# A hybrid attention and HGRN2 block: the output projection by Strassen's seven products from the second tile of positions on

## The reference, cut to what matters

```python
h = rmsnorm(x, w_norm_pre)
proj = h @ w_in                         # (2048, 1024) @ (1024, 3328)
q_a, k_a, v_a, z_a, q_r, f_r, i_r, z_r = split(proj)
o_a = sliding_window_sink_attention(rope(q_a), rope(k_a), v_a, sinks) * silu(z_a)   # 512 columns
o_r = rmsnorm(hgrn2_chunkwise(q_r, f_r, i_r, lb)) * silu(z_r)                       # 512 columns
y = concatenate([o_a, o_r]) @ w_out     # (2048, 1024) @ (1024, 1024)
x = x + rmsnorm(y, w_norm_post)
```

## Time and profile before

| what | value |
|---|---|
| time, median of 3 runs | 876.72 us (874.83 to 877.73) |
| the profiled execution | span 872.4 us from first to last instruction; its own time is not listed apart from the three runs |
| median of the runs less the span | 4.3 us |
| PE busy | 862.6 us, 4478 matmuls |
| DVE, ACT, POOL busy | 592.9, 499.3, 115.7 us |
| DMA | 186 MB, mean 213 GB/s |

### The profile page before, as it was taken

How to read it: one execution, slowest core, us unless ns; L and a number is a source line. 1 busy time by engine, 2 the same in 40 slices (tenths; PEclk the granted TensorE clock), 3 DMA queues, 4 the chain that set the end, 5 groups by cost and what they waited for, 6 DMA issues and landing times.

```text
span 872.4 us, 12348 instructions
## 1 busy us (share of the span) xinstructions
PE 862.6 (99%) x4478; PEld 709.9 (81%) x4478; DVE 592.9 (68%) x1061; ACT 499.3 (57%) x1009; POOL 115.7 (13%) x90
## 2 busy tenths in 40 slices
PE   8999999999999999999999999999999999999997
PEld 6887788888888788888888878888888877788886
DVE  6878867764756798867163679878625468977823
ACT  7766456663574559657147546866624655667532
POOL 0000013430200001342020000243111000013112
PEclk9999999999999999999999999999999999999999
DMA  8685755639968544552785644446379545444463
GB/s 319 236 307 205 265 199 180 250 145 365 418 229 286 221 170 145 177 185 99 289 328 201 241 172 166 146 146 211 130 262 338 193 147 176 154 151 146 161 245 126
DMA packets 52924, 186.03 MB, mean 213 GB/s; under 512 B 5888, under 2 KB 6144, under 8 KB 52864
## 3 DMA queue, kind: packets, MB, share of 16 engines
q1 hardware_dynamic: 50128, 178.29, 57.2%
q10 hardware_dynamic: 2736, 6.95, 2.0%
HBM read 141.18 MB, written 44.04 MB: 212 GB/s over the span
## 4 chain that ended last, share of the span: by engine, by line
PE 88%; DVE 5%; DMA 3%; ACT 2%; issue 1%; SPq 1%; POOL 0%; DVEq 0%; ACTq 0%
PE bank L478 61%; PE bank L487 8%; PE score_b L487 4%; PE turn_b L487 4%; DMA kept_lo<-w_lo 2%; PE score_b L507 2%; PE turn_b L531 2%; PE turn_b L584 2%; PE bank L565 2%; PE turn_b L587 1%; PE bank L575 1%; DVE q_gate L1305 1%; PE turn_b L521 1%; DMA x_in<-in_x 1%; DVE w_lo L997 1%
## 5 line engine op out<-in xcount | busy, mean ns | idle before, releaser
L478 PE MATMUL bank<-h_hi,w_lo 128*128 128x512 f32 x832 | 327.1, 393 | 0.0
L478 PE MATMUL bank<-h_lo,w_hi 128*128 128x512 f32 x832 | 325.9, 392 | 0.0
L478 PE MATMUL bank<-h_hi,w_hi 128*128 128x512 f32 x832 | 324.5, 391 | 0.8 <-ACT h_hi L790 0.8
L478 PEld LDWEIGHTS bank<-h_lo,w_hi 128*128 128x128 f32 x832 | 156.3, 188 | 34.5 <-issue 3.3
L478 PEld LDWEIGHTS bank<-h_hi,w_hi 128*128 128x128 f32 x832 | 156.3, 188 | 33.6 <-ACT h_hi L790 1.3
L478 PEld LDWEIGHTS bank<-h_hi,w_lo 128*128 128x128 f32 x832 | 156.2, 188 | 33.1 <-issue 0.2
L1341 POOL TENSOR_TENSOR mix_lo<-v_r,mix_hi 128x512 fp32r<-128x512 f32 x16 | 21.2, 1323 | 522.6 <-ACT v_r L911 522.6
L997 DVE TENSOR_TENSOR w_lo<-w_raw,w_hi 128x1024 fp32r<-128x1024 f32 x37 | 45.8, 1248 | 32.8 <-ACT w_hi L736 32.6
L1119 DVE STREAM_TRANSPOSE kv_tok<-k_mid 32x128 f32<-32x128 f32 x192 | 58.0, 302 | 2.8
L736 ACT ACTIVATE w_hi<-w_raw 128x1024 fp32r<-128x1024 f32 x38 | 39.7, 1050 | 22.1 <-issue 9.9
L487 PE MATMUL bank<-w_hi,mix_lo 128*128 128x512 f32 x128 | 50.5, 395 | 0.0
(11 more groups left out here) (189 smaller groups left out, 1467.4 us busy)
## 6 DMA issues: line engine op xcount, KB each, us to landing
w_hi<-kept_hi SPq DMA_DIRECT2D x96, 512.0 KB, 3.7
w_lo<-kept_lo SPq DMA_DIRECT2D x96, 512.0 KB, 4.7
w_raw<-in_weights SPq DMA_DIRECT2D x38, 512.0 KB, 5.4
kept_hi<-w_hi SPq DMA_DIRECT2D x34, 512.0 KB, 6.5
kept_lo<-w_lo SPq DMA_DIRECT2D x34, 512.0 KB, 7.1
x_in<-in_x_rows SPq DMA_DIRECT2D x8, 1024.0 KB, 7.2
x_in<-in_x SPq DMA_DIRECT2D x15, 512.0 KB, 5.9
out<-q_gate ACTq DMA_DIRECT2D x9, 512.0 KB, 8.5
```

Of the source, the lines that this page charges most:

```text
L478: mm = pe.matmul(acc(w)[:, :], stationary[:, s, k, :], moving[:, k, :], start=(m == 0), stop=(m == 3 * KT - 1), skip_group_check=True)
```

## The change

Tile 0 is as before. From tile 1 on the 512 positions and the 1024 inputs and 1024 outputs are halved, so that the product is one of 2 by 2 blocks, and seven products of halves take the place of eight. The code has Winograd's form of it, with sums that run on in the banks. `s_hi`, `s_lo` hold three sums of the recurrent and attention halves (S1, S2, S4), `mix_hi[:, 0:4]` the half A11 and the difference S3; they take over the place of `w_raw` in SBUF (with two more slots' room). Of the weights, B11, B21, B12, B22 and four differences T1 to T4 are needed: 14 weight tiles of 1 MiB (high and low) for a tile's output in place of 8, in the order P1A, P1B, P7A, P7B, P2A, P6A, P4A, P2B, P6B, P4B, P5A, P5B, P3A, P3B. The differences are made once, in tile 1, by POOL and ACT from raw weights (`load_sums`, `sum_weights`, `sums_high`) and saved to DRAM (`save_sums`).

One unit is the 3 matmuls of one k block and one 128 positions; there are 56 units (168 matmuls) for a tile. P2B, P6B and P4B are interleaved; P3 finishes the first 128 positions of a half before the second.

```diff
+FAST_ROWS = [B11, B11 + 1, T3, T3 + 1, B21, T2, T4, B21 + 1, T2 + 1, T4 + 1, T1, T1 + 1, B22, B22 + 1]
+FAST_WT = OUT0 + len(FAST_ROWS)
+SPLIT_SLOT = SPLIT_SLOT + [w % 4 for w in range(FAST_WT)] * (TILES - FAST)
+UNITS = [(w, k, i) for w, ks in ((P1A, (0, 1)), (P1B, (2, 3)), (P7A, (0, 1)), (P7B, (2, 3)), (P2A, (0, 1)), (P6A, (0, 1)), (P4A, (0, 1)))
+         for k in ks for i in range(2)]
+UNITS += [(w, k, i) for k in (2, 3) for w in (P2B, P6B, P4B) for i in range(2)]
+UNITS += [(P5A, k, i) for k in (0, 1) for i in range(2)] + [(P5B, k, i) for i in range(2) for k in (2, 3)]
+UNITS += [(w, k, i) for i in range(2) for w, ks in ((P3A, (0, 1)), (P3B, (2, 3))) for k in ks]
...
+SUMS_IN, SUMS_OUT = (6, 13), (11, 18)
+SUMS_AT = (5, 11)
...
+            def load_sums(j):
+
+                if j == 0:
+                    sp.wait_ge(lo_split.sem, lo_split.after(0, 0) + FRESH - 1)
+                else:
+                    sp.wait_ge(t_saved, 16 * T_TILES)
+                for r, w in enumerate((B11, B21, B12, B22)):
+                    sp.dma_start(w_raw[:, r, :, :], weights[(w + j) * P:(w + j + 1) * P, :].rearrange("p (k m) -> p k m", k=KT)).then_inc(t_raw, 16)
+
+            def save_sums(j):
+
+                sp.wait_ge(t_high, 4 * (j + 1))
+                sp.wait_ge(t_low, 4 * (j + 1))
...
-                    if w == WT - 3:
+                    if t == FAST and w in SUMS_IN:
+                        load_sums(SUMS_IN.index(w))
+                    if t == FAST and w in SUMS_OUT:
+                        save_sums(SUMS_OUT.index(w))
+                    if w == (P3A if t >= FAST else WT - 3):
                         load_residual(t, 0)
-                    if w == WT - 1:
+                    if w == tiles_of(t) - 1:
                         load_residual(t, 1)
...
+            def out_fast(t):
+
+                for n, (w, k, i) in enumerate(UNITS):
+                    for part, mix, weight, into in unit(t, w, k, i):
+                        m = 3 * n + part
+                        between(t, OUT0 + m // 21, m % 21)
+                        if part == 0:
+                            unit_waits(t, n, w, k, i)
+                        mm = pe.matmul(into, mix, weight, start=w in (P1A, P7A, P2A, P4A) and k == 0 and part == 0,
+                                       stop=k == KT // 2 - 1 and part == 2, skip_group_check=True)
+                    if w not in [v for v, _, _ in UNITS[n + 1:]]:
+                        mm.then_inc(tile_done.sem, 1)
+                    elif w in (P6B, P5B, P3B) and k == KT // 2 - 1 and i == 0:
+                        mm.then_inc(half_done.sem, 1)
...
+            def sum_head(t, h):
...
+                dve.tensor_tensor(s_tmp[:, S2, :], h_mix[:, 2 * P:], s3[:, h, :], ALU.subtract).then_inc(s_step, 1)
+                dve.tensor_tensor(s_tmp[:, S1, :], h_mix[:, 2 * P:], a21[:, h, :], ALU.add)
+                dve.wait_ge(s_step, (t - FAST) * HEADS + h + 1)
+                dve.tensor_tensor(s_tmp[:, S4, :], h_mix[:, 0:2 * P], s_tmp[:, S2, :], ALU.subtract).then_inc(s_made.sem, 1)
...
+            def sum_weights(j):
+
+                raw = lambda r: w_raw[:, r, :, :]
+                pool.wait_ge(t_raw, 64 * (j + 1))
+                for k, (dst, a, b) in enumerate(((0, 2, 0), (2, 3, 2), (3, 3, 0), (1, 1, 3))):
+                    if k > 1:
+                        pool.wait_ge(t_sum, 4 * j + k)
+                    pool.tensor_tensor(raw(dst), raw(a), raw(b), ALU.subtract).then_inc(t_sum, 1)
+                for k, r in enumerate((0, 2, 3, 1)):
+                    pool.wait_ge(t_high, 4 * j + k + 1)
```

More of the change, by code:

```diff
@@ L57, with index, where, tiles_of @@
 SPLIT_SLOT = [s for r in (4, 4, 4, 4, 4, 4, 4, 3, 3) for s in range(r)]
[L58 to L59 removed]
+FAST = 1
+T_TILES = 8
+B11, B21, B12, B22 = OUT0, OUT0 + 2, OUT0 + 4, OUT0 + 6
+T1, T3, T2, T4 = WT, WT + 2, WT + 4, WT + 6
+P1A, P1B, P7A, P7B, P2A, P6A, P4A, P2B, P6B, P4B, P5A, P5B, P3A, P3B = range(OUT0, OUT0 + 14)
+FAST_ROWS = [B11, B11 + 1, T3, T3 + 1, B21, T2, T4, B21 + 1, T2 + 1, T4 + 1, T1, T1 + 1, B22, B22 + 1]
+FAST_WT = OUT0 + len(FAST_ROWS)
+SPLIT_SLOT = SPLIT_SLOT + [w % 4 for w in range(FAST_WT)] * (TILES - FAST)
+assert WT == 34 and OUT0 == 26 and FAST_WT % 4 == 0 and FAST == 1
+UNITS = [(w, k, i) for w, ks in ((P1A, (0, 1)), (P1B, (2, 3)), (P7A, (0, 1)), (P7B, (2, 3)), (P2A, (0, 1)), (P6A, (0, 1)), (P4A, (0, 1)))
[3 more added lines that the diff above has]
+UNITS += [(w, k, i) for i in range(2) for w, ks in ((P3A, (0, 1)), (P3B, (2, 3))) for k in ks]
+S1, S2, S4 = range(3)
+def index(t, w):
+    return w if t == 0 else WT + (t - FAST) * FAST_WT + w
+def where(i):
+    return (0, i) if i < WT else (FAST + (i - WT) // FAST_WT, (i - WT) % FAST_WT)
+def tiles_of(t):
+    return WT if t < FAST else FAST_WT
+def rows_of(t, w):
+    return FAST_ROWS[w - OUT0] if t >= FAST and w >= OUT0 else w
 SCORES0 = Z0 + 2
@@ L307, in wait_slot @@
                 return
-            tile, v = divmod(before(i), WT)
-            if v in (OUT0 + 3, WT - 1):
+            tile, v = where(before(i))
+            if tile >= FAST:
+                engine.wait_ge(tile_done.sem, tile_done.after(tile, v))
+            elif v in (OUT0 + 3, WT - 1):
                 engine.wait_ge(y_done.sem, y_done.after(tile, 3 if v == OUT0 + 3 else 7))
@@ new lines, in unit @@
+            def unit(t, w, k, i):
+                even, odd = slice(i * P, (i + 1) * P), slice((2 + i) * P, (3 + i) * P)
+                if w in (P1A, P1B, P7A, P7B):
+                    cols = even if w in (P1A, P1B) else odd
+                    hi, lo = mix_hi[:, k, cols], mix_lo[:, k, cols]
+                elif w in (P2A, P2B, P4A, P4B):
+                    cols = even if w in (P2A, P2B) else odd
+                    hi, lo = mix_hi[:, QT + k, cols], mix_lo[:, QT + k, cols]
+                else:
+                    which = S2 if w in (P6A, P6B) else S1 if w in (P5A, P5B) else S4
+                    hi, lo = s_hi[:, which, k, even], s_lo[:, which, k, even]
+                into = w_bank if w in (P7A, P7B) else y_pair if w in (P2A, P2B) else v_bank if w in (P4A, P4B) else x_bank
+                slot, half = SPLIT_SLOT[index(t, w)], slice(4 * (k % 2), 4 * (k % 2) + 4)
+                for part in range(3):
+                    mix, weight = ((hi, w_hi), (lo, w_hi), (hi, w_lo))[part]
+                    yield part, mix, weight[:, slot, half, :].rearrange("p a m -> p (a m)"), into[i][:, :] if len(into[i].shape) == 2 else into[i]
@@ L901, in _ @@
                             place_probs(t, 3, 8)
+                    if t >= FAST and s == out_step(HEADS - 1):
+                        act.wait_ge(tile_done.sem, tile_done.after(t, P1B))
+                        for i in range(2):
+                            keep(t, i, x_bank[i], p1[i])
                     for head in range(HEADS):
```

381 lines of the change are left out of this document (294 added, 87 removed).

## The result

The kernel took **905.97 us** (median of 4 runs, 903.42 to 907.85), against 876.3 (4 runs) in the same series for the kernel before: a ratio of 1.0333, 95% interval [1.0308, 1.0358], slower. The forecast was 881.0, its range ended at 889. The profiled execution took 907.85 us with a span of 906.0, 33.6 above the span before.

A forecast was written before the change was run, and what follows sets the result against it. The prediction took PE's matmuls to bound the kernel, with weight transfers feeding it. Terms -16.3 + 15.3 + 3.9 + 1.5 = +4.4 us on the 872.4 span gave 876.8; runs lie 4.3 higher, so 881 us, range 866 to 889 (8 in 10).

The forecast's parts named there:

- 72 x 0.227 = 16.3 us less: Output projections of three tiles: 192 matmuls become 168 in each, every one removed worth 0.227 us.
- Costed at nothing: The `took`, `keep` and head sums, priced at zero as covered by idle DVE and ACT between 420 and 436 us.
- P3B waits 3.9 us: Output projection: the residual queued ahead of P3B's weights makes them land at 13.4 us, wanted at 9.52.
- rival 1: Output projection: the residual doesn't hold P3B up, which lands 0.7 us late; 869 us, faster; chance 0.19.
- w = 0 waits 1.8 us: Next tile's first weights: behind the second residual they land at 19.3 us, wanted at 17.5; none in the last tile.
- The whole term of 15.3: Waits for weights at P3B and w = 0 over three tiles: 2 x 5.7 + 3.9 = 15.3 us more (10.2 to 18.6).
- Tile 1's start, 3.9 us: Raw loads ahead of the first save delay the save-and-load chain 5.2 us: waits of 3.1 at w = 8, 0.8 at w = 9.
- Together 1.5 us (0 to 6): Making the sums in tile 1: 0.5 us lateness at w = 12 and 1.0 us for DVE held beside POOL.
- Rival 3: The clock falls during PE's wait for P3B: 888 us; chance 0.17, shared with further DVE waits in tile 1.

The follow-up runs named there:

- e11: The changed kernel with the residual behind the next tile's first weights, DVE's last posts ahead of its addition, and no weight sums made: 872.99 us (0.9973).
- e14: e11 with half the bytes in each weight load of the output projections of tiles 1 to 3: 867.25 us (0.9896).
- e5: e1 with DVE's last two posts and the low half of the sum of squares before its wait for the residual, tiles 1 and 2: 890.43 us (1.017).
- e1: The changed kernel with the residual loads moved behind the loads of the next tile's w = 0 and 1: 905.33 us (1.0341).
- e3: The changed kernel with the sums' raw loads and saves kept, but no POOL or ACT work on them: 896.21 us (1.0238).
- e10: e3 with ACT's eight roundings put back, waiting for the raw loads only, without POOL's subtractions: 898.14 us (1.0257).
- e13: e11 with DVE's three head-sum additions for each head cut to two columns: 872.08 us (0.995).
- e6: The changed kernel with 14 unused matmuls per tile ahead of PE's wait for P3B: 904.42 us (1.0329).

## Why the prediction was wrong

Its direction was right, its size was not: +4.4 us forecast, +29.7 found. By its own steps:

- **"72 x 0.227 = 16.3 us less"**: the matmuls are gone, but the value holds only "as long as whatever fed PE at the old pace can feed it at the new one", and I then took the plain weights as fed. **This step failed.** With the residual out of the way the outputs (e11) are 45.4, 44.9 and 50.5 against 47.2, 47.2 and 52.6 before: 6.2 us less in all, not 16.3. I had written that the plain weights "barely keep up" and priced that at zero. e14 shows 6.3 us of it to be the queue; the other 4 or so stay open. In the input stages of tiles 1 and 2 the change loses another 4.4 us that I hadn't counted (see "Costed at nothing"), so that 2.0 us of the 16.3 are left.
- **P3B waits 3.9 us**: measured 3.74, 3.46 and some 3.5. Right, place and size, and rival 1 falls: with the residual away (e5) the wait is 0.9. **w = 0 waits 1.8 us**: not there. P3A waited 0.9 instead, and PE, at half clock behind P3B in tiles 1 and 2, reached w = 0 later than I had it. The whole term of 15.3 is 13.8 to 15.5 by e5, where I had no half clock and one wait too many; that agreement owes something to chance.
- **Tile 1's start, 3.9 us**: w = 8 waited 3.27 (forecast 3.1), w = 7 0.65 (none), w = 9 none (0.8), w = 12 0.88 (0.5). The waits were right; in other executions of the same tile they lay elsewhere by some tenths (e1: w = 7 0.8, w = 9 0.5). What they drew after them was not: 6.8 us at half clock from 276.4 us on. In e3 it was 3.4 us, and the transfers measure 7.7 with it.
- **"Together 1.5 us (0 to 6)" for the making of the sums**: the second large error; POOL and ACT cost 9.8, 8 us more than I gave them. I had the row that shows a held instruction and bounded the loss by one or two holds, because "PE shows no wait there". But DVE was busy 41.3 of 45 us, and it took three holds in a row within 8 us to eat the slack. And I didn't price ACT's roundings as a wait on POOL that stands ahead of others' work in its order; the roundings without that wait are 1.9 (e10).
- **"Costed at nothing"**: `took` and `keep` cost little (e14). The head sums don't lie in the cover that I named, the quiet second half of the output projection (420 to 436 us before): the change has two of the four at 373 and 401 us, in the input stage, and the others at 428 and 439, with the output projection only begun at 417. Of 4.4 us lost in two input stages 2.5 are theirs (e13).
- **Rival 3, the clock falls during the wait**: it did, at P3B in two tiles of three and at three places in tile 1. At P3B it costs a few tenths to 1.8 us a tile (e6), where I had 2.3 to 4.1. In tile 1 there are 17.1 us at half clock; PE was at work in 13.3 of them, a loss of some 6.7 us, with no queue to hide it. I had given it 0.17, and priced it at P3B alone; the waits on DVE in tile 1, which that case names too, did come. The matmul of 0.77 us that I took for one at half clock stands ahead of the first clock that the profile lists (7.4 us), so its clock isn't shown; those at half clock in the change take 0.63 and start every 0.43, 0.20 more than at full.

The range failed since its upper end came from bounds of single holds and single waits: none of it let several engines be late at once. In tile 1's input PE's waits are 4.8 (DMA), 2.7 (DVE), 5.1 (ACT) and 1.2 in two small ones, 13.7 in all; the half clock's 6.7 leave 1 of the stage's 21.5.

On the holds there is a rule. The trace shows two-input DVE operations from SBUF held (L1535, L1398, L1400), and a `TENSOR_SCALAR` with one (L1323, 1.91 us in place of 0.29), while the reduction, the reciprocal, the transposes and the operation that reads a bank (L1558, 0.68 us) beside the same POOL work keep their times. The Trainium skill ("GPSIMD Engine Reference", section "1. Specifications") says that GpSimd shares its SBUF interfaces with VectorE and contends with instructions that have two SBUF inputs or run in a mode with two ports. The trace agrees for the first kind; which mode L1323 ran in it doesn't show. That section gives no price; here it is the rest of the running POOL instruction, up to 2.06 us for an operation of 0.12 beside POOL instructions of 2.4 to 3.2.
